# Rotary row swap: small DMAs issued by ScalarE in place of a TensorE product with a permutation

## The chip, the cores and the metric

The kernel runs on one core of one Trainium2 chip. The time is the device time of one execution in microseconds (us). The core has a matrix engine (TensorE, PE in the profile, with weight loads as PEld), a vector engine (VectorE, DVE), an activation engine (ScalarE, ACT), a general one (GpSimd, POOL) and a queue engine (SyncE, SP). DMAs are issued by SP and by ACT.

## The reference, cut to what matters

The program is three transformer blocks on 512 tokens with a width of 1024, one after the other. The change lies in the first one. There, queries and keys come out of one projection, and a quarter of each head of 64 rows is rotated (eight rows against eight others):

```
def apply_partial_rope(t, cos, sin):
    half = ROPE_DIM // 2          # ROPE_DIM = HEAD_DIM // 4 = 16
    t1 = t[..., :half]
    t2 = t[..., half:ROPE_DIM]
    return jnp.concatenate([t1 * c - t2 * s, t2 * c + t1 * s, t[..., ROPE_DIM:]], axis=-1)
```

Beside it, the same block runs a causal depthwise convolution with 31 taps over 1024 channels, which is independent of the attention until much later.

## The kernel before

Activations lie with channels on partitions (128 at a time) and the 512 tokens along the free dimension. All large products have the same form: a *unit* multiplies one 128-column slice of a weight matrix (1024 x 128) with the activations. The weights are float32, and each is split in a high part `w_hi` and a rest `w_lo`, so that a unit is 24 matmuls (8 slices of the contraction, three products each; L2442, L2443 and L2444 in `three`). All units of the program form one stream with two buffers, numbered U: SP loads `raw[U % 2]`, ACT makes `w_hi` of it (`split_hi`, L542), POOL makes `w_lo` (`low_half`, L421), PE multiplies. ACT may begin the split of a unit when PE has finished the unit two before it, since that frees the buffer; it does so after it has read the finished unit's result.

The stage in question is `qk`: sixteen units j = 0 to 15, one for each 128-row chunk of queries and keys in the order `QK_ORDER` (keys first: 12, 13, 14, 15, 8 to 11, then the queries 0 to 7). It is followed by `token_major` (five units). The engines work in it from orders that are written out by hand:

- PE: unit j (`unit`), then the swap of the chunk before (`swap`, L2628): a product of a 128 x 128 permutation with the chunk, into bank 2 or 3. The last swap stands behind the first unit of `token_major`. Chunks 14 and 15 are not rotated, so there are 14 swaps.
- ACT: read the result of unit j from PSUM into `QK` (L818), then, for j = 4 to 7, issue four DMAs that copy keys (`pairs_of_positions`, L810 and L811), for j = 8, 10, 12 and 14 one that loads weights (`keys_weights`, L804), then `split_hi` of unit j + 2, as the next turn of the loop begins.
- DVE: in slot j of its own loop the rotation `rope` of the chunk of unit j - 2 (three instructions, L1767, L1768 and L1770), for j = 10 to 13 also eight instructions of the compression (`blocks_with_positions`, L1758), then `BESIDE[j]` convolution steps (`conv_taps`, L1740, L1742 and L1738). Behind the loop come the last two ropes, copies, the low halves of the queries (L1798) with convolution steps between them, four copies of masks (L1806), and the low half of the compressed keys (L1808), which waits for a result of ACT. The first 186 of 248 convolution steps (`EARLY`) are done on DVE by then.

Of the kernel before, what the change touches and what calls it, by code (L numbers as in the profile page):

```python
# [11 lines left out]
ALU = mybir.AluOpType  # L12
# [4 lines left out]
S = 512  # L17
# [4 lines left out]
NH, DH, NKV = 16, 64, 4  # L22
GROUP = NH // NKV
TAPS = 31
QK_ORDER = [12, 13, 14, 15, 8, 9, 10, 11, 0, 1, 2, 3, 4, 5, 6, 7]
ROPED = [n for n in QK_ORDER if n < 14]
# [99 lines left out]
def build(nc, t, out, blocks=(1, 2, 3)):  # L126
    ctx = ExitStack()
    FIRST, COUNT, LAST, n_units = plan(blocks)
    with ctx:
# [7 lines left out]
        bank = [psum[:, 512 * i:512 * i + 512] for i in range(8)]  # L137
# [28 lines left out]
        def const(block, name, n=1, i=0):  # L166
            at = CONSTS[block][0][name] + i
            return cst[:, at:at + n]
# [45 lines left out]
        QK = region(16 * S).rearrange("p (c t) -> p c t", t=S)  # L214
# [14 lines left out]

        SCR = region(4 * S)  # L230
        COS, SIN = SCR[:, 0:S], SCR[:, S:2 * S]
        CONV_GATE = QK[:, 8:16]
        SHIFTED_1 = QK[:, 0:8]
        PT = SCR.rearrange("p (b a t) -> p b a t", b=2, a=2)
# [78 lines left out]
        def sw_keys(g, parity):  # L313
# [11 lines left out]
        act_read, dve_read = sem("act_read"), sem("dve_read")  # L325
# [4 lines left out]
        dve_step, act_step = sem("dve_step"), sem("act_step")  # L330
        pad_cleared, conv_tap, conv_done, tap_scaled = (
            sem(n) for n in ("pad_cleared", "conv_tap", "conv_done", "tap_scaled"))
        rope_table, swapped, roped = sem("rope_table"), sem("swapped"), sem("roped")
# [81 lines left out]
        def _(pool):  # L415
            if 1 in blocks:
                pool.memset(Z[:, :, 0:TAPS - 1], 0.0).then_inc(pad_cleared, 1)

            def low_half(U, u):
                pool.wait_ge(w_hi_ready, U + 1)  # L420
# [98 lines left out]
        def _(a):  # L519
            c = Count()  # L520
# [230 lines left out]
            def block_1():  # L751
# [51 lines left out]
                def keys_weights(n):  # L803
                    a.dma_start(CW1K[:, 4 * n:4 * n + 4].rearrange("p c n -> p (c n)"), t["cw1k"][:, 1024 * n:1024 * n + 1024])\  # L804
                     .then_inc(early_in, 16)

                def pairs_of_positions(m, g):

                    src = QK[(g % 2) * DH:(g % 2) * DH + DH, 12 + 2 * m + g // 2, :]
                    a.dma_start(X[0:DH, 4 * m + g, :], src).then_inc(pair_keys_in, 16)  # L810
                    a.dma_start(X[DH:P, 4 * m + g, 0:S - 1], src[:, 1:S]).then_inc(pair_keys_in, 16)  # L811

                for j, chunk in enumerate(QK_ORDER):
                    U = FIRST["qk"] + j
                    if j:
                        split_hi(U + 1, (U + 1) % 2)
                    a.wait_ge(mm_done, U + 1)
                    a.activation(QK[:, chunk], bank[U % 2][:], ACT.Copy, scale=DH ** -0.5 if chunk < 8 else 1.0).then_inc(act_read, 1)  # L818
                    if 4 <= j < 8:
                        a.wait_ge(roped, 2)  # L820
                        for g in (2 * (j % 2), 2 * (j % 2) + 1):
                            pairs_of_positions((j - 4) // 2, g)
                    if j >= 8 and j % 2 == 0:
                        keys_weights((j - 8) // 2)
# [117 lines left out]
                base = c["centered"]  # L942
# [445 lines left out]
        def _(v):  # L1388
            c = Count()

            def link(ins):

                ins.then_inc(dve_step, 1)
                v.wait_ge(dve_step, c.add("step"))
# [255 lines left out]
            def block_1():  # L1650
# [74 lines left out]
                def conv_taps(first, end, acc_of):  # L1725

                    for n in range(first, end):
                        i, j, b = n // (2 * TAPS), n % (2 * TAPS) // 2, n % 2
                        k = 2 * i + b
                        src, acc, w = Z[:, k, j:j + S], acc_of(b), col(1, "conv_w", TAPS * k + j)  # L1730
                        if j:
                            v.wait_ge(conv_tap, 2 * (TAPS - 1) * i + 2 * j + b - 1)
                        else:
                            v.wait_ge(dve_read, k + 1)
                            if i:
                                v.wait_ge(conv_done, 2 * i + b - 1)
                        if j == 0:
                            v.tensor_scalar(acc, src, w, col(1, "conv_b", k), ALU.mult, ALU.add).then_inc(conv_tap, 1)  # L1738
                        elif j < TAPS - 1:
                            v.scalar_tensor_tensor(acc, src, w, acc, ALU.mult, ALU.add).then_inc(conv_tap, 1)  # L1740
                        else:
                            v.scalar_tensor_tensor(src, src, w, acc, ALU.mult, ALU.add).then_inc(conv_done, 1)  # L1742

                in_psum = lambda b: bank[4 + b][:]
                EARLY, PER_GATE = KT * TAPS * 3 // 4, 15
                v.wait_ge(pad_cleared, 1)
                for i in range(2, KT):
                    conv_gate(i)
                    if i < KT - 1:
# [2 lines left out]
                taken = PER_GATE * (KT - 3)  # L1752
# [10 lines left out]
                def rope(k):  # L1763

                    chunk, swapped_k = ROPED[k], bank[2 + k % 2][:]
                    v.wait_ge(swapped, k + 1)
                    v.tensor_tensor(swapped_k, swapped_k, SIN, ALU.mult).then_inc(dve_step, 1)  # L1767
                    v.tensor_tensor(QK[:, chunk], QK[:, chunk], bank[7][:] if k < 12 else COS, ALU.mult).then_inc(dve_step, 1)  # L1768
                    v.wait_ge(dve_step, c.add("step", 2))
                    v.tensor_tensor(QK[:, chunk], QK[:, chunk], swapped_k, ALU.add).then_inc(roped, 1)  # L1770

                BESIDE = (7, 7, 5, 6, 9, 10, 7, 6, 6, 6, 2, 2, 2, 2, 6, 6)
                for j in range(16):
                    if j == 1:
                        v.wait_ge(rope_table, 4)
                        link(v.tensor_scalar(SIN, SIN, const(1, "rope_s"), None, ALU.mult))
                    with_rope = j >= 2 and QK_ORDER[j - 2] < 14
                    if with_rope:
                        rope(ROPED.index(QK_ORDER[j - 2]))
                    if 10 <= j < 14:  # L1780
                        blocks_with_positions((j - 10) // 2, j % 2)
                    conv_taps(taken, taken + BESIDE[j], in_psum)
                    taken += BESIDE[j]
                rope(12)
# [9 lines left out]
                for i in range(8):  # L1794
                    v.wait_ge(q_hi_made, i + 1)
                    for h in (14 - 2 * i, 15 - 2 * i):
                        hi, lo, raw_q = query_parts(h)
                        ins = v.tensor_tensor(lo, raw_q, hi.bitcast(F32), ALU.subtract)  # L1798
                    ins.then_inc(q_lo_made, 1)
                    n = -(-(EARLY - taken) // (8 - i))  # L1800
                    conv_taps(taken, taken + n, in_psum)
                    taken += n
                for dst, name, width in ((IDENT_R, "ident", P), (CAUSAL_R, "causal", P), (CAUSAL_2R[:, P:], "causal", P),
                                         (CMP_MASK_R.rearrange("p (q n) -> p q n", q=TT)[:, :, 0:NCMP], "cmp_mask", TT * NCMP)):
                    src = const(1, name, width)
                    v.tensor_copy(dst, src if width == P else src.rearrange("p (q n) -> p q n", q=TT)).then_inc(masks_made, 1)  # L1806
                v.wait_ge(kc_hi_made, 1)
                v.tensor_tensor(KC_R[:, 1, :, 0:NCMP], bank[6][:, 0:124].rearrange("p (g n) -> p g n", g=NKV),  # L1808
                                KC_R[:, 0, :, 0:NCMP].bitcast(F32), ALU.subtract).then_inc(cmp_ready, 1)
# [95 lines left out]
                with v.Fori(0, 4) as i:  # L1905
                    for u in range(2):
                        n = 2 * i + u
# [529 lines left out]
        def _(pe):  # L2437
            c = Count()
# [182 lines left out]
            def block_1():  # L2621
                conv_gates()
                pe.wait_ge(params_in, c.add("params", 16 * 5))
                def swap(k):

                    if k >= 2:
                        pe.wait_ge(roped, k - 1)
                    pe.matmul(bank[2 + k % 2][:], const(1, "swap", 128), QK[:, ROPED[k]], start=True, stop=True).then_inc(swapped, 1)  # L2628

                first, base = FIRST["qk"], c["act_read"]  # L2630
                banks_free(True)
                for j in range(16):
                    if j == 1:
                        other_bank_free()
                    pe.wait_ge(act_read, base + max(j - 1, 0))
                    unit(first + j, (first + j) % 2, A)
                    if j and QK_ORDER[j - 1] < 14:
                        pe.wait_ge(act_read, base + j)
                        swap(ROPED.index(QK_ORDER[j - 1]))
                c.add("act_read", 16)  # L2640
                last["reader"] = "act_read"
                def last_swap():
                    pe.wait_ge(act_read, c["act_read"])
                    swap(13)
                token_major("token_major", 5, lambda k: last_swap() if k == 0 else None)

                def turn_hidden(m):

# [38 lines left out]
                for g in range(NKV):  # L2687
                    for mt in range(2):
                        ins = pe.matmul(bank[7][0:NCMP, g * DH:(g + 1) * DH], HID[:, 1, mt, g * NCMP:(g + 1) * NCMP], CW2V[:, mt],
                                        start=mt == 0, stop=mt == 1)  # L2690
# [691 lines left out]
```

## Time and profile before

| | us |
|---|---|
| median of 3 runs | 2831.44 |
| lowest, highest | 2829.13, 2832.07 |
| the profiled execution | 2829.63 |
| its span, first to last instruction | 2827.8 |

The profile's times are counted from the span's start. 1.8 us of the execution lie around the span, and the profiled execution is 1.8 us faster than the median. The stage `qk` begins at about 108.7 us, and the last swap ends at about 214.4 us.

### The profile page before, as it was taken

How to read it: one execution, taken by the hardware profiler on the slowest of the kernel's cores; microseconds unless marked ns; L12 is line 12 of the kernel's file. 1: busy time of each engine (PE TensorE's matmuls, PEld its weight loads, DVE VectorE, ACT ScalarE, POOL GpSimd, SP SyncE). 2: the span in 40 equal slices, each digit the busy share in tenths (PEclk: the TensorE clock that was granted, in tenths of full speed). 3: DMA queues.
4: the chain of work that ended last, by engine and by line, in shares of the span. 5: the costliest groups of instructions: out<-in, count | busy, mean ns of one | idle time of the engine just before them, and what ended most of it. 6: DMA issues, size and time to landing. Idle time of an engine off the chain costs nothing.

```text
span 2827.8 us, 38230 instructions
## 1 busy us (share of the span) xinstructions
PE 2722.6 (96%) x13198; PEld 2245.9 (79%) x13198; DVE 1601.2 (57%) x2550; ACT 1018.6 (36%) x1765; POOL 1170.0 (41%) x585
## 2 busy tenths in 40 slices
PE   7999999999999999989999999999899999999997
PEld 6877888778888878878887688888687778888885
DVE  7996767574343376456666645536623447653364
ACT  4325655533222254443334411112525553211133
POOL 3432585244444444344423344444442214444443
PEclk9999999999999999999999999999999999999999
DMA  3342000133222233221102332222231112322322
GB/s 133 102 136 82 17 23 9 47 125 101 95 96 96 97 119 100 82 85 66 60 31 90 113 110 94 97 96 94 93 109 56 45 45 97 126 94 95 95 96 89
DMA packets 67316, 242.90 MB, mean 86 GB/s; under 512 B 7755, under 2 KB 10100, under 8 KB 66428
## 3 DMA queue, kind: packets, MB, share of 16 engines
q1 hardware_dynamic: 59472, 214.32, 23.2%
q10 hardware_dynamic: 7724, 26.96, 2.7%
q8 instruction: 78, 1.28, 0.2%
q14 instruction: 42, 0.34, 0.0%
HBM read 232.80 MB, written 6.35 MB: 85 GB/s over the span
## 4 chain that ended last, share of the span: by engine, by line
issue 46%; PE 36%; POOL 14%; DVE 2%; ACT 1%; POOLq 0%; DMA 0%; DVEq 0%; SPq 0%; ACTq 0%
POOL w_lo L421 12%; PE bank L2442 9%; PE bank L2444 9%; PE bank L2443 9%; PE bank L2984 2%; PE bank L2973 2%; PE bank L2767 1%; POOL stat L448 1%; POOL stat L445 1%; PE bank L2657 0%; PE bank L2754 0%; PE bank L2628 0%; DVE big L1828 0%; PE bank L2715 0%; PE bank L2716 0%
## 5 line engine op out<-in xcount | busy, mean ns | idle before, releaser
L421 POOL TENSOR_TENSOR w_lo<-raw,w_hi 128x1024 fp32r<-128x1024 f32 x398 | 973.1, 2445 | 1586.6 <-ACT w_hi L542 1451.8
L2442 PE MATMUL bank<-act,w_hi 128*128 128x512 f32 x3128 | 1260.6, 403 | 57.9 <-POOL w_lo L421 15.3
L2444 PE MATMUL bank<-act,w_lo 128*128 128x512 f32 x3128 | 1227.0, 392 | 0.0
L2443 PE MATMUL bank<-act,w_hi 128*128 128x512 f32 x3128 | 1226.2, 392 | 0.0
L2442 PEld LDWEIGHTS bank<-act,w_hi 128*128 128x128 f32 x3128 | 592.4, 189 | 208.4 <-issue 30.9
L542 ACT CAST w_hi<-raw 128x1024 fp32r<-128x1024 f32 x396 | 415.5, 1049 | 913.2 <-PE bank L2444 890.8
L2444 PEld LDWEIGHTS bank<-act,w_lo 128*128 128x128 f32 x3128 | 591.9, 189 | 126.9
L2443 PEld LDWEIGHTS bank<-act,w_hi 128*128 128x128 f32 x3128 | 593.2, 190 | 120.4 <-issue 5.5
L1588 DVE TENSOR_TENSOR X<-X,bank 128x512 f32 x56 | 38.5, 688 | 241.4 <-PE bank L2444 241.4
L1970 DVE CAST act<-tmp 128x512 f32 x64 | 138.8, 2169 | 10.0 <-DVE tmp L1966 5.2
L1740 DVE SCALAR_TENSOR_TENSOR bank<-big,cols,bank 128x512 f32<-128x512 f32 x174 | 117.0, 749 | 0.4
L2767 PE MATMUL bank<-big 128*128 128x64 f32 x640 | 82.1, 276 | 12.5 <-DVE big L1841 12.3
L2767 PEld LDWEIGHTS bank<-big 128*128 128x128 f32 x640 | 77.6, 194 | 16.8 <-issue 14.3
L905 ACT ACTIVATE tmp<-bank,big 128x128 f32<-128x128 f32 (+3 forms) x128 | 66.7, 530 | 41.2 <-DVE big L1828 35.1
L1828 DVE TENSOR_REDUCE big<-bank 128x2 f32<-128x256 f32 (+1 forms) x64 | 52.6, 822 | 45.9 <-PE bank L2717 45.8
L448 POOL TENSOR_TENSOR stat<-stat 128x512 f32<-128x512 f32 x58 | 73.9, 1274 | 4.8
L1635 DVE TENSOR_TENSOR tmp<-bank,stat 128x512 f32<-128x512 f32 x22 | 15.2, 692 | 104.9 <-PE bank L2444 104.9
L2337 DVE SCALAR_TENSOR_TENSOR big<-bank,stat 128x128 f32<-128x128 f32 (+3 forms) x32 | 15.7, 491 | 92.6 <-ACT stat L1316 92.6
L915 ACT COPY big<-bank 128x128 f32<-128x128 f32 (+3 forms) x128 | 48.3, 431 | 54.8 <-PE bank L2754 54.7
L2973 PEld LDWEIGHTS bank<-big 128*128 128x128 f32 x384 | 51.0, 194 | 16.1 <-ACT tmp L1119 6.2
L2131 DVE TENSOR_TENSOR stat<-bank,cst 128x256 f32<-128x256 f32 x96 | 40.7, 424 | 40.0 <-PE bank L2973 38.1
L2973 PE MATMUL bank<-big 128*128 128x128 f32 x384 | 54.7, 284 | 8.8 <-ACT tmp L1119 5.8
(397 smaller groups left out, 2929.1 us busy)
## 6 DMA issues: line engine op xcount, KB each, us to landing
raw<-in_w_dram SPq DMA_DIRECT2D x402, 512.0 KB, 3.5
act_f<-head_rows ACTq DMA_DIRECT2D x8, 768.0 KB, 4.1
proj_rows<-big ACTq DMA_DIRECT2D x4, 1024.0 KB, 4.1
big<-proj_rows ACTq DMA_DIRECT2D x2, 2048.0 KB, 10.4
X<-in_x_dram SPq DMA_DIRECT2D x4, 512.0 KB, 6.2
act_f<-in_cw1k_dram ACTq DMA_DIRECT2D x4, 512.0 KB, 4.1
out_dram<-X ACTq DMA_DIRECT2D x4, 512.0 KB, 2.7
cst<-in_consts_dram ACTq DMA_DIRECT2D x2, 648.5 KB, 8.9
```

The costliest lines, as they stand in the source:

```text
L421: pool.tensor_tensor(w_lo[:, u], raw[:, u].rearrange("p (k n) -> p k n", k=KT), w_hi[:, u].bitcast(F32), ALU.subtract).then_inc(w_lo_ready, 1)
L448: pool.tensor_tensor(to, acc, product, ALU.add).then_inc(done, 1)
L542: a.copy(w_hi[:, u].rearrange("p k n -> p (k n)"), raw[:, u]).then_inc(w_hi_ready, 1)
L905: a.activation(by_tile(tmp[:, 2 * b + j, 0:kw]), score_branches(n)[:, j], ACT.Exp, bias=MX[:, b, j:j + 1], accum_out=SUMS[:, n % 4, j:j + ...
L1740: v.scalar_tensor_tensor(acc, src, w, acc, ALU.mult, ALU.add).then_inc(conv_tap, 1)
L1970: v.tensor_copy(hi, y).then_inc(hi_made, 1)
L2442: pe.matmul(o, l_hi, r_hi, start=start, stop=False)
L2443: pe.matmul(o, l_hi, r_lo, start=False, stop=False)
L2444: return pe.matmul(o, l_lo, r_hi, start=False, stop=stop)
L2767: pe.matmul(o[:, j], PT[:, b, j, k * P:k * P + P], V_TOK[:, 2 * j + g // 2, k, (g % 2) * DH:(g % 2) * DH + DH], start=k == 0, stop=k == qt)
L2973: ins = pe.matmul(bank[2 + half][:, quad[j]], MT[:, 2 * half + j], TM[:, 2 * half + j], start=True, stop=True)
L2984: ins = pe.matmul(bank[4 + half][:, quad[j]], XM[:, 2 * half + j], UM[h % 2][:, 2 * half + j], start=True, stop=True)
```

## The change

It takes the 14 swaps out of PE's order. In their place ACT, after it has read chunk j, issues four DMAs (L820 of the new file) that copy 8 rows of 512 tokens each within SBUF, into a new area `SWAPPED` with two halves; the other rows of it are cleared once at the start. The rope waits for these DMAs, and multiplies `SWAPPED` with the sines; the sines are copied to PSUM bank 6 for it. The counts `BESIDE` are changed, so that 13 convolution steps leave the `qk` loop; three of them now stand between the low halves of the queries and ten behind the copies of the masks.

```
+        SWAPPED = SCR[:, 2 * S:4 * S].rearrange("p (b t) -> p b t", b=2)
+        TURN = 8
...
                 pool.memset(Z[:, :, 0:TAPS - 1], 0.0).then_inc(pad_cleared, 1)
+                pool.memset(SWAPPED, 0.0).then_inc(pad_cleared, 1)
...
+                def swap_halves(k):
+
+                    a.wait_ge(act_read, c["read"] + QK_ORDER.index(ROPED[k]) + 1)
+                    if k:
+                        a.wait_ge(swapped, 64 * k)
+                    if k >= 2:
+                        a.wait_ge(roped, k - 1)
+                    for row in (0, DH):
+                        for half in (0, TURN):
+                            to, other = row + half, row + TURN - half
+                            a.dma_start(SWAPPED[to:to + TURN, k % 2], QK[other:other + TURN, ROPED[k]]).then_inc(swapped, 16)
...
                     a.activation(QK[:, chunk], bank[U % 2][:], ACT.Copy, scale=DH ** -0.5 if chunk < 8 else 1.0).then_inc(act_read, 1)
+                    if j == 0:
+                        a.wait_ge(pad_cleared, 2)
+                    if chunk < 14:
+                        swap_halves(ROPED.index(chunk))
...
-                    v.wait_ge(swapped, k + 1)
-                    v.tensor_tensor(swapped_k, swapped_k, SIN, ALU.mult).then_inc(dve_step, 1)
+                    v.wait_ge(swapped, 64 * (k + 1))
+                    v.tensor_tensor(swapped_k, SWAPPED[:, k % 2], bank[6][:] if k < 12 else SIN, ALU.mult).then_inc(dve_step, 1)
...
-                BESIDE = (7, 7, 5, 6, 9, 10, 7, 6, 6, 6, 2, 2, 2, 2, 6, 6)
+                BESIDE = (8, 8, 5, 5, 8, 8, 5, 5, 5, 5, 1, 1, 1, 1, 5, 5)
...
+                        link(v.tensor_copy(bank[6][:], SIN))
...
-                    n = -(-(EARLY - taken) // (8 - i))
-                    conv_taps(taken, taken + n, in_psum)
-                    taken += n
+                    conv_taps(taken, taken + 2, in_psum)
+                    taken += 2
...
+                conv_taps(taken, EARLY, in_psum)
                 v.wait_ge(kc_hi_made, 1)
...
-                def swap(k):
-
-                    if k >= 2:
-                        pe.wait_ge(roped, k - 1)
-                    pe.matmul(bank[2 + k % 2][:], const(1, "swap", 128), QK[:, ROPED[k]], start=True, stop=True).then_inc(swapped, 1)
-
...
-                    if j and QK_ORDER[j - 1] < 14:
-                        pe.wait_ge(act_read, base + j)
-                        swap(ROPED.index(QK_ORDER[j - 1]))
...
-                token_major("token_major", 5, lambda k: last_swap() if k == 0 else None)
+                token_major("token_major", 5, lambda k: pe.wait_ge(roped, 12) if k == 0 else None)
```

On ScalarE's queue, the turns of units 12 and 13 read so before (L818 reads a result, L804 loads weights, L542 splits the weights of the unit after the next):

```order
L818 ACTIVATE big<-bank 128x512 [waits mm_done]
L804 DMA act_f<-in_cw1k_dram 128x1024
L542 CAST w_hi<-raw 128x1024 [waits mm_done,w_loaded_even]
L818 ACTIVATE big<-bank 128x512 [waits mm_done]
L542 CAST w_hi<-raw 128x1024 [waits mm_done,w_loaded_odd]
```

The same two turns after the change, where L833 is the read, L820 the row copies, L807 the load and L545 the split:

```order
L833 ACTIVATE big<-bank 128x512 [waits mm_done]
L820 DMA big<-big 8x512 [waits roped,swapped,act_read]
L820 DMA big<-big 8x512 x3
L807 DMA act_f<-in_cw1k_dram 128x1024
L545 CAST w_hi<-raw 128x1024 [waits mm_done,w_loaded_even]
L833 ACTIVATE big<-bank 128x512 [waits mm_done]
L820 DMA big<-big 8x512 [waits roped,swapped,act_read]
L820 DMA big<-big 8x512 x3
L545 CAST w_hi<-raw 128x1024 [waits mm_done,w_loaded_odd]
```

Four DMA issues now stand between the read and the split, and the first of them waits for the read to be complete (`act_read`). For j = 4 to 7 they stand ahead of the four DMAs of `pairs_of_positions`.

On VectorE's queue, the end of the query halves before the change (L1798 the low halves, L1740 and L1742 convolution steps, L1806 the masks, L1808 the compressed keys):

```order
L1798 TENSOR_TENSOR big_r<-X,big_r 64x512 [waits q_hi_made]
L1798 TENSOR_TENSOR big_r<-X,big_r 64x512
L1742 SCALAR_TENSOR_TENSOR big<-big,cols,bank 128x512 [waits conv_tap]
L1806 CAST big_r<-cst 128x128 x3
L1806 CAST big_r<-cst 128x4x31
L1808 TENSOR_TENSOR big_r<-bank,big_r 128x4x31 [waits kc_hi_made]
```

And the same place after it (L1818, L1759 and L1761, L1825 and L1828 in that order):

```order
L1818 TENSOR_TENSOR big_r<-X,big_r 64x512 [waits q_hi_made]
L1818 TENSOR_TENSOR big_r<-X,big_r 64x512
L1759 SCALAR_TENSOR_TENSOR bank<-big,cols,bank 128x512 [waits conv_tap] x2
L1825 CAST big_r<-cst 128x128 x3
L1825 CAST big_r<-cst 128x4x31
L1759 SCALAR_TENSOR_TENSOR bank<-big,cols,bank 128x512 [waits conv_tap] x8
L1761 SCALAR_TENSOR_TENSOR big<-big,cols,bank 128x512 [waits conv_tap] x2
L1828 TENSOR_TENSOR big_r<-bank,big_r 128x4x31 [waits kc_hi_made]
```

Ten convolution steps now stand between the masks and the instruction that waits for ACT.

## Rows read from the trace of the kernel before

**Rows 1.** The page, part 1: busy time, share of the span, instructions.
```profile
PE 2722.6 (96%) x13198; PEld 2245.9 (79%) x13198; DVE 1601.2 (57%) x2550; ACT 1018.6 (36%) x1765; POOL 1170.0 (41%) x585
```

**Rows 2.** Timeline of ACT and POOL: start, us, engine, line, idle before.
```profile
114.22 0.60 ACT L818 ACTIVATE big<-bank 128x512 f32<-128x512 f32 x1 [0.62 <-PE bank L2444]
...
119.67 0.60 ACT L818 ACTIVATE big<-bank 128x512 f32<-128x512 f32 x1 [3.92 <-PE bank L2444]
...
181.76 0.60 ACT L818 ACTIVATE big<-bank 128x512 f32<-128x512 f32 x1 [4.84 <-PE bank L2444]
182.25 1.04 ACT L542 CAST w_hi<-raw 128x1024 fp32r<-128x1024 f32 x1
183.37 2.40 POOL L421 TENSOR_TENSOR w_lo<-raw,w_hi 128x1024 fp32r<-128x1024 f32 x1 [3.97 <-ACT w_hi L542]
188.13 0.60 ACT L818 ACTIVATE big<-bank 128x512 f32<-128x512 f32 x1 [4.83 <-PE bank L2444]
...
207.84 1.28 ACT L557 ACT_TABLE_LOAD   x1
...
219.96 0.60 ACT L679 ACTIVATE stat<-bank 128x512 f32<-128x512 f32 x1 [4.83 <-PE bank L2444]
```

**Rows 3.** Timeline of ACT in the turn of unit 5, with its DMA issues (ACTq).
```profile
143.29 0.60 ACT L818 ACTIVATE big<-bank 128x512 f32<-128x512 f32 x1 [1.67 <-PE bank L2444]
143.29 0.49 ACTq L810 DMA_DIRECT2D X<-big  x1
...
144.46 0.62 ACTq L810 DMA_DIRECT2D X<-big  x1
145.11 0.62 ACTq L811 DMA_DIRECT2D X<-big  x1
145.82 1.05 ACT L542 CAST w_hi<-raw 128x1024 fp32r<-128x1024 f32 x1 [1.94 <-issue]
```

**Rows 4.** Timeline of ACT around 2045 us: other small DMA issues.
```profile
2045.36 0.44 ACTq L1280 DMA_DIRECT2D big<-in_rel_dram  x1
2045.83 0.40 ACTq L1281 DMA_DIRECT2D big<-in_bucket_dram  x1
...
2051.22 0.28 ACTq L1289 DMA_DIRECT2D bias_rows<-big  x1
```

**Rows 5.** Timeline of PE: two waits (in brackets) and the matmul behind each.
```profile
573.18 0.47 PE L2442 MATMUL bank<-act,w_hi 128*128 128x512 f32 x1 [2.58 <-POOL w_lo L421]
...
1553.09 0.80 PE L2442 MATMUL bank<-act,w_hi 128*128 128x512 f32 x1 [3.99 <-DVE act L2223]
```

**Rows 6.** Stretches behind these waits; last three columns granted clock, DMA share, GB/s.
```profile
573.00:577.00 4.00, 3.82 (x15) 2.66 (x15) 2.07 (x4) 3.24 (x4) 0.00 (x0) 1.00 0.36 131
...
1553.00:1557.00 4.00, 3.91 (x9) 3.14 (x10) 0.72 (x2) 1.04 (x1) 1.05 (x1) 0.50 0.12 48
```

**Rows 7.** Timeline of DVE: eight instructions of compression, a rope, six steps.
```profile
184.54 3.05 DVE L1758 TENSOR_SCALAR act_f<-X,cols 128x124 f32<-128x124 f32 x8
...
195.35 0.70 DVE L1767 TENSOR_TENSOR bank<-bank,big 128x512 f32<-128x512 f32 x1
...
197.28 4.04 DVE L1740 SCALAR_TENSOR_TENSOR bank<-big,cols,bank 128x512 f32<-128x512 f32 x6
```

**Rows 8.** Timeline of DVE behind the query halves.
```profile
247.36 0.62 DVE L1806 CAST big_r<-cst 128x128 fp32r<-128x128 f32 x4
...
254.84 0.29 DVE L1808 TENSOR_TENSOR big_r<-bank,big_r 128x124 fp32r<-128x124 f32 x1 [6.85 <-ACT big_r L865]
...
261.26 1.80 DVE L1816 TENSOR_TENSOR act<-X,act 64x512 fp32r<-64x512 f32 x1 [6.14 <-ACT act L840]
```

**Rows 9.** Groups by line and form: a memset of 1024 columns, busy us and mean ns.
```profile
L505 POOL MEMSET big<- 128x1024 f32 x2 | 1.9, 960 | 0.0
```

**Rows 10.** Timeline of POOL at the start.
```profile
5.62 2.35 POOL L421 TENSOR_TENSOR w_lo<-raw,w_hi 128x1024 fp32r<-128x1024 f32 x1 [4.57 <-ACT w_hi L754]
```

**Rows 11.** The page, part 6: a 64-row copy of `pairs_of_positions`, median us to landing.
```profile
X<-big ACTq DMA_DIRECT2D x8, 128.0 KB, 3.2
```

More of the change, by code:

```diff
@@ L1745, in block_1 @@
                 EARLY, PER_GATE = KT * TAPS * 3 // 4, 15
-                v.wait_ge(pad_cleared, 1)
+                v.wait_ge(pad_cleared, 2)
                 for i in range(2, KT):
@@ L2636, in block_1 @@
                     unit(first + j, (first + j) % 2, A)
-                    if j and QK_ORDER[j - 1] < 14:
-                        pe.wait_ge(act_read, base + j)
-                        swap(ROPED.index(QK_ORDER[j - 1]))
                 c.add("act_read", 16)
                 last["reader"] = "act_read"
-                def last_swap():
-                    pe.wait_ge(act_read, c["act_read"])
-                    swap(13)
-                token_major("token_major", 5, lambda k: last_swap() if k == 0 else None)
+                token_major("token_major", 5, lambda k: pe.wait_ge(roped, 12) if k == 0 else None)
                 def turn_hidden(m):
```

## Prediction

> **What bounds the kernel now.** I read the page's busy line first [rows 1]: TensorE is busy for 96% of the span, so what matters is whether an edit shortens TensorE's order or makes it wait. Then I went to the stage `qk` in the timelines. Units without a swap behind them follow each other at 5.45 us (119.67 - 114.22, the reads of units 0 and 1), units with one at 6.37 us (188.13 - 181.76) [rows 2]. A swap thus costs 0.92 us of TensorE's order. From the read of unit 0 to that of the second unit of `token_major` (219.96, unit 17 in what follows) are 105.74 us; 17 units take 92.65 of them, and the 14 swaps 13.1.
>
> TensorE does not wait here, because the weights of unit n + 2 are ready in time. Their chain starts when unit n ends: ScalarE reads the result 0.04 us later (0.60 us), the split begins 0.49 us behind the start of that read and overlaps its end, and takes 1.04; GpSimd starts 0.08 later and takes 2.40, done at 185.77, while TensorE needs the result after 188 [rows 2]. VectorE is busy nearly without a gap in this stage, but nothing waits for it yet.
>
> **The change part by part.**
>
> *Removed: the 14 swaps.* They give back 13.1 us if nothing else moves.
>
> *Added: 56 DMA issues on ScalarE's queue, between the read and the split.* This is the term that decides. Such issues block the split: behind unit 5's read, four of them end only at 145.73, and the split starts at 145.82 instead of 143.78 [rows 3]. They start together with the read, the new ones only behind its end, since they wait for `act_read`. Let d be the time from one row copy's issue to the next. Then the weights for unit n + 2 are ready, counted from the end of unit n, at
>
> R = 0.04 + 0.60 (read) + 0.04 (hand-over) + 4d + 0.09 (last issue to split) + 1.04 + 0.08 + 2.40 + 0.12 (hand-over to TensorE) = 4.41 + 4d.
>
> The hand-overs of 0.04, 0.12 are read off similar places and matter little. For units 4 to 7 the pair copies, now queued themselves, add 2.63 us (four times the spacing from 144.46 to 145.11, 0.65, is 2.60, and one issue in this stage was longer) [rows 3]; for 8, 10, 12 and 14 a weight load adds 0.44, the time of a queued issue [rows 4]; for unit 15 a table load adds 1.28 [rows 2]. Units 2 and 3 have no row copies. Unit n + 2 starts at the end of unit n + 1 or at the end of unit n plus R, whichever is later. TensorE therefore waits as soon as R is over 5.45, that is, from d = 0.26 on; a late start in one turn gives the next chain more time, so that a pair of turns loses R - 5.45 about once, not twice.
>
> *The size of d* is not in the trace. The nearest rows are: 0.28 us for a single issue of eight rows to DRAM, 0.44 and 0.40 for queued ones of 32 and 33 rows from DRAM [rows 4], and 0.65 from issue to issue for the 64-row copies within SBUF, the same kind of transfer as the new ones [rows 3]. The bounds are 0.28 and 0.65. For the lower end speaks the number of rows, eight; for the upper, that four stand in a queue and that both ends lie in SBUF. I take 0.50. The waits that follow from the rule above, before unit: 2: 0.96; 6: 3.59; 7: 0.95; 8: 2.64; 9: 0.95; 10: 0.45; 11: 0.51; 12: 0.89; 13: 0.07; 14: 1.33; 16: 1.40; 17: 0.84. Together 14.6 us. As an example, unit 4 ends 22.74 us after unit 0, unit 5 at 28.19, and unit 6 may start at 22.74 + 4.41 + 2.00 + 2.63 = 31.78: a wait of 3.59. The balance is 14.6 - 13.1 = +1.5 us. With d = 0.28 the waits are 8.4 us (-4.7), with 0.65 they are 19.0 (+5.9).
>
> The Trainium skill (DMA: Bandwidth & Descriptors, section Issuing engines are not separate DMA queues) says that the sequencer's time for initiating a DMA is "usually small relative to the DMA itself". For the 64-row copies the trace has 0.62 us of issue beside 3.2 us to landing [rows 3, 11], a fifth, and it is the issue that the split waits for. Taken at its word for this sum, the rule would make 4d nearly nothing; that is the first rival below.
>
> *The clock.* A wait of 2.58 us left the granted clock at 1.00, and one of 3.99 us was followed by a stretch at 0.50, the lower of its two levels [rows 5, 6]. Four us at 0.50 cost 2 us. The wait of 3.59 us before unit 6 lies between the two, nearer to the second. I add half of 2 us, +1.0, for it.
>
> *The landing of the copies* is hidden as long as VectorE comes late to its ropes. With 3.2 us from issue to landing [rows 11] a chunk is swapped 0.7 + 3d + 3.2, so about 5.4 us after its unit's end; the slot that needs it begins later still, since VectorE's slots 0 and 1 now hold sixteen steps and a copy, 16 x 0.66 + 0.6 = 11.2 us, and begin when unit 0 does, 5.45 us before its end: the first rope's turn comes 5.8 us after that end. If that cover were gone, VectorE would wait 1 to 2 us per slot, and only then would ScalarE's new wait for `roped` bite, behind which the split is queued.
>
> *VectorE's slots.* The rope takes 1.93 us (195.35 to 197.28), a convolution step 0.66 to 0.67, the compression 3.05 [rows 7]. The new slots are 1.93 + 5 x 0.66 = 5.2 us, with compression 1.93 + 3.05 + 0.7 = 5.7; a unit with its wait takes 6.3 on average. So VectorE keeps up, and ScalarE's wait for the rope two turns back costs nothing. The copy of the sines adds one instruction of some 0.6 us once, to a slot without a rope.
>
> *The ten steps behind the masks* take 10 x 0.67 = 6.7 us, the three between the halves 2. VectorE sat idle for 6.85 us before the compressed keys, and 6.14 us before its next instruction [rows 8]. At worst the keys' low half is some 2 us late, and the idle time behind it takes that up: nothing.
>
> *The memset* of 128 x 1024 on GpSimd costs 0.96 us [rows 9], at the start, where the engine waited for 4.57 us before its first low half [rows 10]: nothing.
>
> **Sum.** -13.1 + 14.6 + 1.0 = +2.5 us. Against the profiled execution of 2829.63 that is 2832.1; the median is 1.8 above it, so that the forecast is 2833.9, which is 0.09% slower. About 0.2%, or 5.7 us, is what a measurement of this kernel can tell from no change.
>
> **The rivals.**
>
> *Issues cost little: faster.* The issue of eight rows is so cheap that only the pair copies still hold the split. For d = 0 the waits are 1.59 + 1.59 + 0.24 = 3.4 us, the change gives 9.7 us, and the time is 2821.8. To leave the band of 0.2% d must be below 0.25 (-5.5). For it speaks the single issue of 0.28 us; against it that no queued issue in the trace was under 0.40 [rows 4]. A chance of 13%; 5 of these are for the case of the Trainium skill's sentence, with d near 0.
>
> *ScalarE becomes the bound of the stage: slower.* If each row copy costs as much as a 64-row one (0.65), the waits are 19.0 us, +5.9, and the one before unit 6 is 4.2 us, longer than the one that was followed by half the clock [rows 5, 6], which adds 2: +7.9, and with the wait before unit 8 in the same way +9.9. That is 2839.3 to 2841.3. It decides from about d = 0.58 on if the clock falls (+3.8 and 2), and from 0.64 alone. For it: it is the same kind of transfer on the same queue. Against it: an eighth of the rows. A chance of 23%.
>
> *The transfers are late instead of the issues.* The copies land later than 3.2 us, beside the weight loads, VectorE waits, and `roped` holds ScalarE. A landing of 6 us would stretch only turns in which TensorE waits already; some 2 us more, 2836. 5%, inside the band mostly.
>
> **Chances and range.** My case, from d = 0.3 to 0.6 with or without one loss of clock, has 60%. Faster by over 0.2%: 13%. Within 0.2%: 62%. Slower: 25%. The range goes from 2826.7 (d = 0.28, no loss of clock) to 2840 (d = 0.65 and one to two losses): about 1 in 10 is left out on either side.
>
> **What the profile after would show.** No L2628. Four row copies behind each read, spaced by d: 0.50. Unit 1's read to unit 2's read 6.4 us instead of 6.37, then alternating turns of 5.45 and about 6.4; waits of TensorE for `w_lo`, the longest, about 3.6 and 2.6 us, before units 6 and 8. VectorE's ropes start without long waits. From the read of unit 0 to unit 17's: 107.2 us plus what the clock takes, where it was 105.74; behind it everything shifted by the same amount. The prediction is wrong if the copies' spacing is under 0.28 or over 0.65, if the granted clock falls in several of these waits, or if a wait shows up behind unit 17 for one of VectorE's results.

## The result and the profile after

The changed kernel takes 2844.33 us (median of 5 runs, 2842.55 to 2848.02), the kernel before, beside it, 2831.44 (5 runs, 2829.13 to 2832.07). The ratio is 1.0053, with a 95% interval of 1.0042 to 1.0064: slower by 12.9 us, outside the predicted range. The profiled execution took 2844.33 us, its span is 2842.5.

The page's busy line of the kernel after, the counterpart of [rows 1]. TensorE has 28 instructions less, the 14 products with the permutation. Its busy time falls by 5.4 us only and not by 13.1, since what follows below, three stretches at half the clock and the restarts behind its waits, counts as busy:

```profile
PE 2717.2 (96%) x13170; PEld 2244.1 (79%) x13170; DVE 1601.1 (56%) x2551; ACT 1019.5 (36%) x1765; POOL 1170.3 (41%) x586
```

From the read of unit 0 to that of unit 17, the timeline of ScalarE after has these two ends. They are 118.88 us apart, where they were 105.74 [rows 2]. The difference, 13.1 us, is nearly all of the loss. The spans of the two profiled executions differ by 14.7; of the other 1.6 us, 0.2 lie ahead of the stage and 1.4 behind it. From unit 17's read to the end the profiled executions of this study take 2607.0 to 2612.3 us, so a difference of 1.4 there can't be told from chance.

```profile
114.42 0.60 ACT L833 ACTIVATE big<-bank 128x512 f32<-128x512 f32 x1 [0.62 <-PE bank L2464]
...
233.30 0.60 ACT L682 ACTIVATE stat<-bank 128x512 f32<-128x512 f32 x1 [4.50 <-PE bank L2464]
```

The same timeline in the turns of units 10 and 11 (L833 is the read, L820 the four row copies of `swap_halves`, L807 a load of `CW1K`, L545 the split; ACTq is ScalarE's sequencer issuing DMAs):

```profile
185.86 0.60 ACT L833 ACTIVATE big<-bank 128x512 f32<-128x512 f32 x1 [3.45 <-PE bank L2464]
186.49 2.61 ACTq L820 DMA_DIRECT2D big<-big  x4
189.14 0.46 ACTq L807 DMA_DIRECT2D act_f<-in_cw1k_dram  x1
189.69 1.05 ACT L545 CAST w_hi<-raw 128x1024 fp32r<-128x1024 f32 x1 [3.23 <-DMA big<-big]
191.30 0.60 ACT L833 ACTIVATE big<-bank 128x512 f32<-128x512 f32 x1 [0.56 <-PE bank L2464]
191.92 2.63 ACTq L820 DMA_DIRECT2D big<-big  x4
194.65 1.04 ACT L545 CAST w_hi<-raw 128x1024 fp32r<-128x1024 f32 x1 [2.76 <-DMA big<-big]
```

Four row copies hold the sequencer for 2.61 to 2.63 us here, 0.65 or 0.66 from one to the next, and the split stands behind them. Where the profile writes "DMA big<-big" as what ended the idle time, read the rows between: the split waits by the program for `mm_done` and the loaded weights, and for no data of these copies; it starts 0.09 or 0.10 us behind the end of the last issue. In the turn of unit 6 the copies of pairs (L825, L826) follow, and ScalarE has no free time between read and read:

```profile
155.59 0.60 ACT L833 ACTIVATE big<-bank 128x512 f32<-128x512 f32 x1 [2.31 <-PE bank L2464]
156.22 2.73 ACTq L820 DMA_DIRECT2D big<-big  x4
158.99 0.56 ACTq L825 DMA_DIRECT2D X<-big  x1
...
160.88 0.62 ACTq L826 DMA_DIRECT2D X<-big  x1
161.59 1.04 ACT L545 CAST w_hi<-raw 128x1024 fp32r<-128x1024 f32 x1 [5.41 <-issue]
162.55 0.59 ACT L833 ACTIVATE big<-bank 128x512 f32<-128x512 f32 x1
```

What TensorE makes of it, in its timeline after: the waits before units 6, 8 and 12, and the matmul behind each.

```profile
148.25 0.47 PE L2462 MATMUL bank<-act,w_hi 128*128 128x512 f32 x1 [4.12 <-POOL w_lo L424]
...
165.21 0.47 PE L2462 MATMUL bank<-act,w_hi 128*128 128x512 f32 x1 [3.59 <-POOL w_lo L424]
...
193.32 0.77 PE L2462 MATMUL bank<-act,w_hi 128*128 128x512 f32 x1 [2.06 <-POOL w_lo L424]
```

The view of waits from 100 to 262 us (us in total, times, longest) adds up nine such waits, all for `w_lo`. It also shows eleven waits of VectorE for the row copies, which are discussed below:

```profile
DVE bank L1786 <- DMA big<-big: 23.9, 11, 4.0
...
PE bank L2462 <- POOL w_lo L424: 19.2, 9, 4.1
```

Three stretches of 3.40 us, one behind each of the three waits shown above, in the view by windows (the third column from the right is the granted clock). TensorE works at 1.2 GHz in them instead of 2.4, so each costs half of its 3.4 us, 1.7:

```profile
148.90:152.30 3.40, 3.40 (x10) 2.62 (x9) 0.00 (x0) 0.07 (x1) 0.00 (x0) 0.50 0.87 236
165.95:169.35 3.40, 3.40 (x9) 2.67 (x8) 0.00 (x0) 0.77 (x1) 0.00 (x0) 0.50 0.86 250
193.25:196.65 3.40, 3.33 (x8) 2.69 (x9) 2.48 (x9) 1.04 (x1) 0.88 (x1) 0.50 0.54 172
```

**The account of the stage.** 17 units take 92.65 us, nine waits 19.2, three falls of the clock 5.1; together 116.95. The other 1.9 us are about 0.2 for each wait, the time of a restart. A wait is counted from the modelled end of the last matmul (0.39 us long), but matmuls in a row follow each other at 0.23: 0.16 us of overlap are lost at every stop, and the first matmul behind a wait, 0.47 long, is followed only 0.30 later instead of 0.23. So a wait of w costs about w + 0.25. This account, 92.65 + waits + 0.25 for each + 1.7 for each fall, comes within 0.4 us of every stage profiled in this study from which the products are gone.

### The profile page after: what moved, and what is told of

It is laid out like the page before. It is cut to its first block, busy times and chain, and to the rows that moved or that the text cites. A ratio compares the mean times of both kernels' runs of the same rounds, so it can differ in the third digit from the quotient of the medians.

```text
span 2842.5 us, 38235 instructions
## 1 busy us (share of the span) xinstructions
PE 2717.2 (96%) x13170; PEld 2244.1 (79%) x13170; DVE 1601.1 (56%) x2551; ACT 1019.5 (36%) x1765; POOL 1170.3 (41%) x586
## 4 chain that ended last, share of the span: by engine, by line
issue 52%; PE 29%; POOL 15%; DVE 2%; ACT 1%; POOLq 1%; DMA 0%; DVEq 0%; ACTq 0%
POOL w_lo L424 14%; PE bank L2462 7%; PE bank L2464 7%; PE bank L2463 7%; PE bank L2992 2%; PE bank L2981 2%; PE bank L2775 1%; POOL stat L451 1%; POOL stat L448 1%; PE bank L2665 0%; PE bank L2762 0%; DVE big L1848 0%; POOLq L428 0%; PE bank L2723 0%; PE bank L2724 0%
## 5 line engine op out<-in xcount | busy, mean ns | idle before, releaser
L545 ACT CAST w_hi<-raw 128x1024 fp32r<-128x1024 f32 x396 | 415.7, 1050 | 953.6 <-PE bank L2464 896.9
L1759 DVE SCALAR_TENSOR_TENSOR bank<-big,cols,bank 128x512 f32<-128x512 f32 x174 | 117.4, 752 | 0.5
```

What stands on the lines that cost most here:

```text
L545: a.copy(w_hi[:, u].rearrange("p k n -> p (k n)"), raw[:, u]).then_inc(w_hi_ready, 1)
```

## The experiments

Times of the kernel before beside the first four runs: 2830.23 us; beside the next four: 2830.27; beside the last: 2829.78. "Stage" is always from the read of unit 0 to that of unit 17, 105.74 us in the kernel before and 118.88 in the changed one. Two theories stood at first. A: the issues of the row copies ahead of the split make the weights late, and this is all. B: something else of the change does it, the copies' traffic or landing, or VectorE's new order.

**The row copies behind the split, still on ScalarE.** `swap_halves` of a chunk is issued behind the next split instead of ahead of it:

```
                     if j:
                         split_hi(U + 1, (U + 1) % 2)
+                    if j and QK_ORDER[j - 1] < 14:
+                        swap_halves(ROPED.index(QK_ORDER[j - 1]))
                     a.wait_ge(mm_done, U + 1)
                     a.activation(QK[:, chunk], bank[U % 2][:], ...)
-                    if chunk < 14:
-                        swap_halves(ROPED.index(chunk))
```

> The changed kernel with one thing moved: ScalarE issues a chunk's row copies behind the split of the next weights, not ahead of it. Theory A (the four issues, 0.66 us each, hold up the split, and with it TensorE): the chain from a unit's end to the weights of the unit after the next is back to 4.2 us in turns without pair copies, and TensorE waits only around units 5 to 9, where a turn of ScalarE takes some 7 us; the stage from the read of unit 0 to that of unit 17 takes about 98 us, where it was 105.7 before and 118.9 with the change, and the time is about 2823. Theory B (the copies land late, or disturb the weight loads, and VectorE's ropes and all that wait for them are late): the copies come another 1 us later, so that nothing is won, 2844 or more.

Measured: 2819.07 us (2817.73 to 2824.19), ratio 0.9965 (0.9951 to 0.9979), stage 98.2 us (from 113.03 to 211.23). ScalarE's timeline of this run shows that the copies now run beside the split, since an issue occupies the sequencer and not the arithmetic:

```profile
161.80 0.60 ACT L837 ACTIVATE big<-bank 128x512 f32<-128x512 f32 x1 [4.44 <-PE bank L2464]
161.81 0.35 ACTq L807 DMA_DIRECT2D act_f<-in_cw1k_dram  x1
162.29 1.04 ACT L545 CAST w_hi<-raw 128x1024 fp32r<-128x1024 f32 x1
162.43 2.63 ACTq L820 DMA_DIRECT2D big<-big  x4
```

The same 56 copies, the same traffic, the same order on VectorE, 25 us less. Theory A: the stage came out as expected, with two waits (0.97 and 2.03 us, before units 6 and 8) and one fall of the clock in it; the median is 4 us under the 2823 that I gave, and the profiled execution took 2822.66.

**The row copies issued by SyncE**, whose queue carries the weight loads and waits most of the time. For each of the sixteen units:

```
+            for j in range(16):
+                if QK_ORDER[j] < 14:
+                    swap_halves(j)
+                load(begin + j, (begin + j) % 2)
```

> The changed kernel with the 56 row copies issued by SyncE, between its weight loads, and none by ScalarE; same data, same waits. Theory A: ScalarE's turns are those of before, TensorE's units follow each other at 5.45 us without a swap, and the stage takes 92.7 us and some 1 to 2 us around the pair copies: 2818 to 2820. Theory B: the transfers are the same and as late as with the change, VectorE waits for them, so that the time stays at 2835 to 2844.

Measured: 2820.62 us (2815.94 to 2821.05), ratio 0.9963 (0.9949 to 0.9976), stage 95.9 us, no fall of the clock in it. The stage is 1.2 us longer and the median 0.6 above what theory A gave; B's 2835 is far off. An issue on SyncE takes about as long as on ScalarE: 0.62 us in the middle of 56, and 2.66 us for most groups of four. What was left, waits of 0.9 and 1.4 us before units 6 and 8, stands where the copies of pairs are ahead of the split.

**Two of the four row copies.** `for half in (0,)`, and 32 in place of 64 in the waits; half of the swapped rows are left out, so that the result is not the reference's.

> The changed kernel with two of the four row copies of each chunk left out, so that half of the rotated rows lack their partner's product. Theory A: two issues less are 1.3 us less per turn, the chain is 5.75 us instead of 7.05, and the waits sum to about 10 us instead of 19: a stage of about 103 us, 105 with a fall of the clock, so 2828 to 2831. Theory B (lateness of the landing, not number of issues): the landing is 1.3 us earlier at most, and the time is over 2838.

Measured: 2832.5 us (2829.41 to 2835.07), ratio 1.0009 (0.9999 to 1.0018), stage 106.7 us. That is 1.5 above the upper end of A's range and 5.5 under B's. The account closes: eight waits of 10.1 us together, 2.0 for the restarts, one fall of the clock 1.7, and 92.65 are 106.5. The expectation's 105 has the fall of the clock in it; what I had left out were the restarts.

**VectorE's moved steps alone.** The kernel before with `BESIDE`, the two steps between query halves and the rest behind the masks as in the changed one.

> The kernel before, with nothing but the convolution steps moved as in the change (three between the query halves, ten behind the masks), and the swaps still on TensorE. Theory A: the moved steps cost nothing, 2831 within 1.5 us. Theory C (the steps in front of the compressed keys' low half delay what follows, and make a part of the 12.9 us): 2833 to 2838.

Measured: 2830.39 us (2828.91 to 2833.0), ratio 1.0003 (0.9993 to 1.0012). The moved steps cost nothing.

**What an issue's time depends on.** The changed kernel, where the four copies of a chunk take another form for every second chunk:

```
+                            if k < 2:      # as they were: 8 rows of 512
+                            elif k < 4:    # 8 rows of 8 numbers
+                            elif k < 6:    # 1 row of 512
+                            elif k < 8:    # 8 rows of 512, from DRAM
+                            elif k < 10:   # 8 rows of 512, to DRAM
+                            elif k < 12:   # 32 rows of 256
+                            else:          # 128 rows of 128
```

> The changed kernel with its 56 row copies in other forms, eight of each, where the first eight are as they were (8 rows of 512, within SBUF, 0.63 to 0.66 us from issue to issue). What it computes in the rotary turn is thereby wrong from the third chunk on; the waits and the number of issues stay. It asks what sets an issue's time. Theory S (both ends in SBUF): every form within SBUF, be it 8 rows of 8 numbers, one row of 512, 32 rows of 256 or 128 rows of 128, takes 0.60 to 0.66 us, and 8 rows from DRAM to SBUF, or from SBUF to DRAM, 0.28 to 0.46. Theory R (rows or bytes): one row, or 8 rows of 8 numbers, is at 0.3 us or below, and 128 rows are above 0.9. Theory Q (the queue): all forms take 0.6 to 0.7 wherever four stand in a row, from and to DRAM too.

ScalarE's timeline of this run, one group of four for each form in the order of the list, without the first, which is the form above, and two issues of the weight load L807, which is the same 128 x 1024 from DRAM each time:

```profile
140.10 2.61 ACTq L824 DMA_DIRECT2D big<-big  x4
...
164.25 2.47 ACTq L826 DMA_DIRECT2D big<-big  x4
...
179.69 1.33 ACTq L828 DMA_DIRECT2D big<-in_x_dram  x4
...
187.70 0.36 ACTq L807 DMA_DIRECT2D act_f<-in_cw1k_dram  x1
...
191.71 1.31 ACTq L830 DMA_DIRECT2D proj_rows<-big  x4
...
203.65 2.45 ACTq L832 DMA_DIRECT2D big<-big  x4
...
214.01 0.62 ACTq L807 DMA_DIRECT2D act_f<-in_cw1k_dram  x1
...
216.92 2.44 ACTq L835 DMA_DIRECT2D big<-big  x4
```

For the copies themselves theory S holds, and R and Q fall. 0.2 KB in eight rows (L824) take 0.65 us an issue (2.61 for four), 64 KB in 128 rows (L835) 0.61. With one end in DRAM the same 8 rows take 0.33 to 0.35. The other group of each form reads 2.73, 3.01, 1.37, 1.41, 2.52 and 2.49, so that only the single row (3.01 once) strays. The row of 0.28 us [rows 4], which I took as a lower bound because of its eight rows, ended in DRAM, and this fits the forms here; its few rows don't explain it. Theory S is not the whole rule, though: the load L807 took 0.47 and 0.36 us behind the copies with an end in DRAM, 0.60 and 0.62 behind those of 32 and of 128 rows, so what stands ahead in the queue counts too. Why, no run shows. In the turns with DRAM copies TensorE had no wait over 1 us. The run's one time was 2840.62 us.

**Only the copies of pairs moved behind the split**, in the changed kernel:

```
                     if j:
                         split_hi(U + 1, (U + 1) % 2)
+                    if 5 <= j < 9:
+                        a.wait_ge(roped, 2)
+                        for g in (2 * ((j - 1) % 2), 2 * ((j - 1) % 2) + 1):
+                            pairs_of_positions((j - 5) // 2, g)
```

> The changed kernel with one thing moved: the 16 copies of pairs of positions, issued between the read and the split in units 4 to 7, stand behind that split. The 56 row copies stay ahead of it. Theory A (the sum of issue times ahead of the split sets the weights' lateness, and the waits of about 4 us set off the falls of the clock): R is some 7.1 us instead of 9.8 in units 4 to 7, but ScalarE's own turn is still 0.6 + 2.65 + 1.04 + 2.6 = about 7.0 there, so that these turns take 7.0 each, 28 for the four where they took 33.8 us (reads at 138.72 and 172.54 of the changed kernel): -5.8, and with one or two falls of the clock less (1.7 each) 2835 to 2837 on the scale on which the changed kernel has 2844.3, and no wait of TensorE over 3 us. Theory B (these issues do no harm of their own, the row copies cost it all): 2842 to 2845, the falls of the clock as before.

Measured: 2834.93 us (2832.49 to 2841.14, 10 runs), ratio 1.0018 (1.0009 to 1.0027), stage 112.3 us. This is 9.4 us under the changed kernel, and at the lower end of theory A's range, far from B's. The ten executions spread over 8.7 us, and the profiled one (2840.86) is among the longest; its stage is 6.6 us shorter than the changed kernel's, and no wait in it is over 3 us. The waits before units 6 to 10 were 1.59, 0.35, 1.08, 0.39 and 1.53 us, where they had been 4.12, 0.35, 3.59, none and 2.16. There were two falls of the clock in the stage, but behind waits of 2.27 and 1.96 us, which stand elsewhere. So the part of theory A that tied the falls to the waits of about 4 us was too narrow.

**SyncE issues the row copies, and the pairs stand behind the split**: both edits above together.

> As the run in which SyncE issues the row copies (2820.6, stage of 95.9 us from the read of unit 0 to unit 17's), and the copies of pairs of positions on ScalarE moved behind the split. Theory A (what was left of the waits came from these pair copies): the stage takes 92.7 to 94 us, no wait of TensorE over 1 us, 2817.5 to 2819. Theory B (it came from SyncE's turn, whose four issues and weight load stand in one queue): 95.5 to 96.5 us, 2820 to 2821.

Measured: 2817.79 us (2814.64 to 2820.96), ratio 0.9957 (0.9943 to 0.9970), stage 92.94 us, no wait of TensorE over 1 us in it. All three are as theory A said.

**The other way round**: row copies on ScalarE behind the split, the copies of pairs on SyncE ahead of a weight load.

```
+                if 4 <= j < 8:
+                    sp.wait_ge(act_read, KT + j + 1)
+                    sp.wait_ge(roped, 2)
+                    for g in (2 * (j % 2), 2 * (j % 2) + 1):
+                        pairs_of_positions((j - 4) // 2, g)
                 load(begin + j, (begin + j) % 2)
```

> The row copies on ScalarE behind the split, and the 16 copies of pairs of positions on SyncE between its weight loads. ScalarE's turn is then 0.6 + 1.04 + 2.65 = 4.3 us everywhere, under the 5.45 of a unit. Theory A (the 98.2 us of the first such run came from the four turns in which both kinds of copies filled ScalarE, 6.9 us each): the stage takes 92.7 to 94 us, 2813.5 to 2816, the clock without a fall there. Theory B (a row copy behind the split is itself late, and VectorE's ropes then hold the order): 96 us or more, waits of VectorE for big<-big, 2817 to 2820.

Measured: 2817.38 us (2816.43 to 2820.42), ratio 0.9957 (0.9943 to 0.9970), 1.4 above theory A's range and inside theory B's; the stage, 92.93 us without a fall of the clock, is theory A's, and B's 96 us did not come. Its ends and three neighbouring rows in ScalarE's timeline:

```profile
114.65 0.60 ACT L851 ACTIVATE big<-bank 128x512 f32<-128x512 f32 x1 [0.62 <-PE bank L2474]
...
147.29 0.60 ACT L851 ACTIVATE big<-bank 128x512 f32<-128x512 f32 x1 [3.90 <-PE bank L2474]
147.78 1.04 ACT L565 CAST w_hi<-raw 128x1024 fp32r<-128x1024 f32 x1
147.91 2.83 ACTq L840 DMA_DIRECT2D big<-big  x4
...
207.58 0.60 ACT L702 ACTIVATE stat<-bank 128x512 f32<-128x512 f32 x1 [4.36 <-PE bank L2474]
```

All four versions with the row copies out of the split's way (2817.4 to 2820.6 us) beat both kernels; this one and the run before it, with the pairs moved too, are the fastest. The stage is 12.8 us shorter than in the kernel before, and the median 12.9: of the 13.1 us of the products all but 0.3 come back, and it was the placing of the issues that had eaten them.

**The changed kernel once more**, to see what repeats.

> The changed kernel as it is, profiled and timed once more, to see what of its stage is fixed and what differs from one execution to the next. Theory A (the waits follow from the program, the falls of the clock depend also on when a wait comes): the waits of TensorE over 1 us stand before the same seven units with the same lengths to 0.1 us, the number of falls in the stage is again two to four and they need not follow the same waits; the stage is 93 + 19 + 2 + 1.7 for each fall, so 117.5 us with two, 119 with three, 121 with four, and the ratio to the kernel before 1.004 to 1.006. Theory B (the clock falls behind the two longest waits, over 3.5 us, and the third fall was chance): those two recur every time and no other.

Measured: 2846.28 us (4 runs, 2843.48 to 2847.68), ratio 1.0055 (1.0039 to 1.0072), stage 118.95 us. The waits over 1 us stand before the same seven units, 2.28, 4.12, 4.17, 2.11, 2.06, 2.06 and 2.27 us long. One differs by more than the 0.1 us of theory A: before unit 8 it is 4.17, where it was 3.59. Again there are three falls, two behind the same two long waits, the third behind the wait before unit 14 instead of 12. Stage, ratio and number of falls are as theory A said; that a third fall came again, and in another place, speaks against B's "no other".

## Why the prediction was wrong

**The mechanism was right.** The swaps cost what was said: without them and without waits 17 units take 92.94 us, where 92.65 was worked out. The bound was TensorE's waits for `w_lo`, through ScalarE's queue. The formula for R holds to about 0.1 us, now with measured issues. Unit 0: 4.41 + 3.27 (its first group of four) = 7.68, and unit 2 begins 7.72 us after unit 0's end. Unit 10: 4.41 + 4 x 0.66 + 0.44 = 7.49, and from its end at 185.83 to the matmul at 193.32 it is 7.49.

**The step that failed: "the size of d".** I took 0.50, between 0.28 and 0.65, because eight rows are an eighth of 64. It measured 0.65 to 0.68 (four in 2.61 to 2.73 us, and 3.27 the first time), the upper bound and a little more. The run with other forms shows why: between two places of SBUF an issue took 0.61 to 0.68 us whatever it carried (0.75 once), and the short row had an end in DRAM. The trace of the kernel before could have said so. In it the load of 128 rows x 1024 from DRAM is issued in 0.34 us, hardly more than the eight rows' 0.28, so that the number of rows was no reason for the lower end:

```profile
162.66 0.34 ACTq L804 DMA_DIRECT2D act_f<-in_cw1k_dram  x1
```

The rule that one waits about once for a pair of turns was right, and for d = 0.65 it had given 19.0 us of waits; 19.2 were measured. So this term alone was 4.6 us too small. The sum agrees, the places do not: the prediction put waits before units 7 and 9 too (0.95 us each), and there were 0.35 and none, while that before unit 8 was 3.59 and not 2.64. A likely reason is that a unit which runs at half the clock for a while takes up the wait that would follow it. By an estimate, the prediction's rule with the measured issues and with units 6, 8 and 12 lengthened by 1.7 us gives 0.1 us before unit 7, none before unit 9, 3.8 before unit 8 and 2.1 before units 10, 12, 14 and 16.

The Trainium skill's sentence on the sequencer's time (DMA: Bandwidth & Descriptors, section Issuing engines are not separate DMA queues) got 5%. For a copy within SBUF an issue of 0.62 us stands beside 3.2 to landing (64 rows) [rows 3, 11], a fifth, so the trace does not contradict it as a share; as a guide for this sum it misleads, since the place of the issues in the queues decided about 27 us (2844.3 against 2817.4).

**The second term, the clock**, was counted as half of one fall of 2 us. Three falls of 1.7 us came, in both profiles of this kernel: 4.1 us too small. I had read from one wait of 2.58 us without a fall [rows 5, 6] that waits of that length are harmless. Waits of 1.96 to 2.9 us were followed by a fall at times.

**A term that was missing**: 0.2 to 0.25 us for each stop of TensorE, 1.9 us in all. Of the 10.4 us between forecast and median, 4.6 + 4.1 + 1.9 = 10.6 are thus named. (The four chances of the prediction's cases, 60, 13, 23 and 5%, add up to 101.)

**The rivals.** "ScalarE becomes the bound: slower", at 23%, is what happened, with d and place as it said. Its 2839.3 to 2841.3 were still 3 us short, for the third fall and the restarts. "Issues cost little" and "the transfers are late" fell: moving the issues, with the transfers the same, removed the loss.

**VectorE.** "The landing is hidden" and "the ropes start without long waits" were wrong in the letter: it waited eleven times for row copies, 23.9 us together. It cost nothing: no wait of TensorE or ScalarE in the stage is put down to VectorE. Its slots of 5.2 us stood in turns that the late weights had stretched to 7.0 on average (118.88 / 17), so that it came early to its ropes. ScalarE never waited for `roped`: each group of row copies begins within 0.1 us of its read's end. With SyncE's issues and full speed of TensorE the same ropes fit in 5.45 us a unit. That is why a wait of 24 us in the view of waits need not be a loss.

**The other parts held.** The ten steps behind the masks: VectorE's timeline after shows them before the low half of the compressed keys (L1828), which has no idle time ahead of it now where it had 6.85 us, and the next instruction still waits for ScalarE, 5.56 us where it was 6.14 [rows 8]:

```profile
262.02 5.36 DVE L1759 SCALAR_TENSOR_TENSOR bank<-big,cols,bank 128x512 f32<-128x512 f32 x8
267.29 1.40 DVE L1761 SCALAR_TENSOR_TENSOR big<-big,cols,bank 128x512 f32<-128x512 f32 x2
268.60 0.28 DVE L1828 TENSOR_TENSOR big_r<-bank,big_r 128x124 fp32r<-128x124 f32 x1
274.45 3.97 DVE L1836 TENSOR_TENSOR act<-X,act 64x512 fp32r<-64x512 f32 x4 [5.56 <-ACT act L859]
```

The run with the steps alone says the same. The memset is hidden as well: in GpSimd's timeline after, the first low half starts 0.04 us later than in [rows 10], and still waits 3.72 us.

```profile
5.66 2.35 POOL L424 TENSOR_TENSOR w_lo<-raw,w_hi 128x1024 fp32r<-128x1024 f32 x1 [3.72 <-ACT w_hi L757]
```

## What to carry to other kernels

A DMA issued by a computing engine is an instruction of that engine's queue: price it by the nearest row with the same two ends (SBUF or DRAM) and a like place in the queue, not by its size, and ask what stands behind it. Put it behind the work that another engine waits for, or on a queue that idles; in this kernel that alone, done for the row copies and the copies of pairs, made 1.0053 into 0.9957. When a sum rests on an unknown between far bounds, ask which property the rows at its ends differ in before choosing a middle, and give each predicted stop of TensorE its restart and the chance of a fall of the clock.

## What the runs showed of the hardware

From one row copy's issue to the next within SBUF it took 0.61 to 0.71 us on ScalarE (once 0.75), for 0.2 KB as for 64 KB, for 8 rows as for 128; with an end in DRAM, 8 rows took 0.33 to 0.35. On SyncE it was 0.67 for most groups of four, and up to 0.79 for some, most of them where ScalarE issued copies at the same time. The first group on ScalarE took 3.27 to 3.31 us instead of 2.4 to 2.8 for four (3.01 once). A few single copies of pairs took 1.2 to 1.9 us instead of 0.6. The load of 128 x 1024 from DRAM took 0.33 to 0.35 us with nothing just ahead of it, 0.46 behind four row copies, and 0.62 behind four copies of 128 rows.

An issue holds up what stands behind it in the queue, and not the arithmetic that was started ahead of it: with the copies behind the split, four issues began 0.14 us after it and ran beside its 1.04 us.

The clock: in the stages of the changed kernel (twice), of the runs with the copies behind the split, with two of four, with the other forms, and with the pairs moved, TensorE had 26 waits of 1.96 us or more and 12 falls. Every fall began within 0.2 us before and 0.8 us after the end of such a wait and lasted 3.4 us. All six waits over 3.5 us were followed by one, and six of the 20 between 1.96 and 2.9. Which of these it is changed from one execution to the next; why, stays open. None of the shorter waits in this stage was followed by a fall. That makes 1.96 us no threshold: behind the stage, in the run with the pairs on SyncE, a fall came with a wait of 1.71 us, a few matmuls behind one of 0.69.
